# GpSimd makes some of the convolution's products itself, and the first layer norm's sums move between projection units

## The chip, the cores and the metric

One Trainium2 chip, one core. The kernel's time is what the core takes for one launch, in microseconds (us); the numbers shown are the median of several runs. The profile is one execution taken by the hardware profiler, with its own time. TensorE is called PE, VectorE DVE, ScalarE ACT and GpSimd POOL in its rows.

## The reference, cut to what matters

Two transformer blocks over 256 rows of 1024 values, all in float32. The change touches only the token mixer of the first block:

```python
z = rmsnorm(x, mix_norm) @ w_in               # 5376 columns: q, k, v, conv a and b, two gates
q, k = rope(rmsnorm(q, q_norm)), rope(rmsnorm(k, k_norm))
a = sliding_window_attention(q, k, v, sinks) @ attn_proj
u = ca * sigmoid(cb)                          # 1024 channels
u = causal_depthwise_conv(u, dw_w, dw_b)      # 31 taps per channel
c = silu(layernorm(u, g, b)) @ conv_proj
x = x + (sigmoid(ga) * a + sigmoid(gb) * c) @ w_out
```

A layer norm needs the sum over the 1024 channels, then the sum of the squared differences from the mean. The channels lie on the partitions, so both sums are matmuls with a matrix of ones.

## The kernel before, in words

**Weights.** All weights are streamed as units of 128 x 1024 values (512 KB) through a ring of 8 buffers `raw`. A float32 product is made from three fast ones: ScalarE writes a rounded copy `w_hi` (L504), VectorE the rest `w_lo` (L948), and TensorE runs w_hi x a_hi, w_lo x a_hi and w_hi x a_lo for each of two row tiles: 12 matmuls of 512 columns for a unit. SyncE loads unit u once TensorE has done unit u-8. `w.to(n)` in ScalarE's and VectorE's programs writes the parts up to unit n+1, so that these engines write parts some five units ahead of TensorE.

**The mixer's 44 steps.** The columns of w_in are taken in 11 blocks of 4 units: conv 0, conv 1, qkv 0, qkv 1, qkv 2 (half as wide), conv 2, conv 3, gate 0 to 3. TensorE's step s uses unit s; ScalarE's and VectorE's slot s is what their programs do beside it (L716 to L764 and L1356 to L1380). After the last unit of a conv block ScalarE makes its sigmoid (`csg`, L754), VectorE the gated product (`cub`, L1352, function `gated_conv`, in slot 4p+3 of block p), TensorE transposes it two steps on (L1979) and ScalarE copies it to `uT` (L727). `Q1` is slot 20 and `A0` slot 31.

**The heads.** VectorE norms and turns q and k in `shape_heads` in slots 20 to 23: the sums of squares, the inverse root (with a square root on ScalarE, for which two activation tables are loaded), products, the rotation (`rope`, L1334), and last `kdup` (L1340), which TensorE's `k_turn` waits for at step 27. Then `kTz` (L1378) is copied from PSUM in slot 28 (`A0 - 3`), which `q_turn(1)` at step 29 waits for. From step 31 on each step holds a group of attention heads: scores on TensorE, maxima on VectorE (L1226), exponentials on ScalarE, transposes and values on TensorE.

**The 31 taps.** Two of the four pairs of 128-channel chunks (`VECT_CH`) are VectorE's: `conv(n)` adds n taps of one chunk each (L1262, accumulating in PSUM), 124 in all. The others (`POOL_CH`) are made in two steps: ScalarE multiplies (`products(n)`, L673, two instructions for a tap of a pair) into one of two buffers `prod`, and GpSimd adds it to `y` (L485). A product may be written once the add two taps before is done (`pool_step`). `TAPS_IN` and the calls of `products` say how many go into each slot.

**The end.** Eight units of attn_proj (`u_ap`), beside them the last taps; then TensorE sums y (L1993 to L1999), VectorE subtracts the mean, ScalarE squares, TensorE sums the squares (L2005), VectorE and ScalarE make the inverse root and the normed, split input, and TensorE starts conv_proj (`u_cp`); `busy(n, bank)` runs n filler matmuls (L1718) in between. The gates' sigmoids (L774) stand between the last products and the squares. After conv_proj VectorE merges the two branches, and w_out (`u_wo`) follows.

Of the kernel before, what the change touches and what calls it, by code (L numbers as in the profile page):

```python
# [25 lines left out]
P = 128  # L26
S = 256
# [60 lines left out]
def two_blocks(nc, A, consts, out):  # L88
    ctx = ExitStack()
    with ctx:  # L90
# [79 lines left out]
        assert e <= END, (e, END)  # L170
        qT, _, _ = place("qT", [P, KC, S], F32, ARENA)
# [181 lines left out]
        ROOTS = ["heads", "ln", "f2_1", "f2_post0", "mix2_0", "f2_post1", "mix2_1", "gla",  # L353
# [19 lines left out]
        POOL_CH = [0, 4]  # L373
        VECT_CH = [2, 6]
# [10 lines left out]
        A2, OA_AT = 3, 4  # L385
        K_BANK, Q_BANKS = 7, [4, 7, 4, 5]
# [51 lines left out]
        def _(pool):  # L438
# [38 lines left out]

            for g in range(2):
                c = POOL_CH[g]
                for k in range(1, TAPS):  # L480
                    j = (TAPS - 1) * g + k - 1
                    pool.wait_ge(sem("conv_product"), TAP2 * g + 2 * (k + 1))
                    if j >= 1:
                        pool.wait_ge(sem("pool_step"), j)
                    pool.tensor_tensor(y[:, c:c + 2, :], y[:, c:c + 2, :], prod[:, j % 2, :, :], ALU.add).then_inc(sem("pool_step"), 1)  # L485
# [13 lines left out]
        def _(act):  # L499
# [156 lines left out]
            made = [0]  # L656

            def products(n, limit=2 * TAP2):

                for i in range(made[0], min(made[0] + n, limit)):  # L660
                    g, k, half = i // TAP2, i % TAP2 // 2, i % 2
                    c = POOL_CH[g] + half
                    src = uT[:, c, k:k + S]
                    if i % TAP2 == 0:
                        act.wait_ge(sem("uT_ready"), 2 + 2 * g)
                    if k == 0:
                        r = ROW[("dw_b", 0)]
                        ins = act.activation(y[:, c, :], src, ACT.Identity, scale=par[:, c, 0:1], bias=par[:, c, r:r + 1])
                    else:
                        j = (TAPS - 1) * g + k - 1  # L670
                        if j >= 2:
                            act.wait_ge(sem("pool_step"), j - 1)
                        ins = act.activation(prod[:, j % 2, half, :], src, ACT.Copy, scale=par[:, c, k:k + 1])  # L673
                    ins.then_inc(sem("conv_product"), 1)
                made[0] = max(made[0], min(made[0] + n, limit))
# [39 lines left out]

            for slot in range(NMIX):  # L716
# [5 lines left out]
                if slot == Q1:  # L722
                    load_table(ACT.Sqrt)
                if i == 2 and p >= 1 and MIX[p - 1][0] == "conv":
                    j = MIX[p - 1][1]
                    act.wait_ge(sem("conv_turned"), j + 1)
                    act.activation(uT[:, 2 * j:2 * j + 2, TAPS - 1:], ps[:, 4 + j % 2, :].rearrange("p (c n) -> p c n", c=2),  # L727
                                   ACT.Copy).then_inc(sem("uT_ready"), 1)
                if A0 - 3 <= slot <= A0:
                    c = slot - A0 + 3  # L730
                    act.wait_ge(sem("q_turned"), c + 1)
                    act.wait_ge(sem("gqT_ready"), 2)
                    act.activation(qT[:, 2 * c:2 * c + 2, :].rearrange("p c n -> p (c n)"), ps[:, Q_BANKS[c], :], ACT.Copy, scale=gqT)\
# [209 lines left out]
        def _(dve):  # L943
# [412 lines left out]
            for slot in range(NMIX):  # L1356
# [5 lines left out]
                if 1 <= a <= NG:  # L1362
                    take_values(a - 1)
# [843 lines left out]
```

## Time and profile before

| | us |
|---|---|
| median of 3 runs | 1440.61 (1435.54 to 1441.94) |
| the profiled execution's own time | 1436.06 |
| its span in the profile | 1434.3 |
| TensorE busy | 1365.7 (95%) |
| VectorE busy | 961.5 (67%) |
| ScalarE busy | 786.1 (55%) |
| GpSimd busy | 142.2 (10%) |

The mixer of the first block runs from about 212 to 463 us of the span. Busy time of TensorE counts modelled ends of pipelined matmuls, so the gaps between its instructions, and the starts of one and the next, say more than its share. The granted clock is a share of 2.4 GHz, and 0.50 is the level of 1.2 GHz.

### The profile page before, as it was taken

Reading aid. Unit: us, or ns where it says so; the run is one execution under the profiler, and the core shown is the slowest. Engines: PE = TensorE matmul, PEld = TensorE weight load, DVE = VectorE, ACT = ScalarE, POOL = GpSimd, SP = SyncE. Lnnn points to the kernel's source line nnn. Section 1 sums busy time; section 2 is a strip of 40 time slices with the busy share of each in tenths; the row PEclk is TensorE's granted clock in tenths of the full one; section 3 lists DMA queues with packets and bytes.
Section 4 is the critical chain, followed back from the end, with each engine's and each line's share of the span. In section 5 each row is a group of like instructions: output and inputs, shape, how many; then the busy total and the mean of one; then the engine's idle time right before and its main releaser. Section 6 shows DMA issues by size and latency. Waiting matters only on the chain.

```text
span 1434.3 us, 17249 instructions
## 1 busy us (share of the span) xinstructions
PE 1365.7 (95%) x6512; PEld 1124.6 (78%) x6512; DVE 961.5 (67%) x1397; ACT 786.1 (55%) x1249; POOL 142.2 (10%) x166
## 2 busy tenths in 40 slices
PE   7999999849998999999999999999999999999997
PEld 5788788638876888878778878788888888688886
DVE  5767746797867776774768766568776546665543
ACT  5444447858874554444674444676545664754442
POOL 4000102733430000010001000000000000000000
PEclk9999999969999999999999999999999999999999
DMA  9888765613343687875558876555544345556662
GB/s 295 295 265 266 262 187 153 203 44 104 103 133 111 190 273 253 282 264 179 174 186 273 272 261 184 164 170 166 150 146 117 103 146 161 159 179 190 182 188 86
DMA packets 166691, 269.60 MB, mean 188 GB/s; under 512 B 14096, under 2 KB 114616, under 8 KB 166608
## 3 DMA queue, kind: packets, MB, share of 16 engines
q1 hardware_dynamic: 154240, 226.66, 50.8%
q0 software_dynamic: 12064, 41.49, 8.5%
q8 instruction: 52, 0.85, 0.2%
q10 hardware_dynamic: 304, 0.35, 0.1%
q14 instruction: 31, 0.25, 0.1%
HBM read 267.40 MB, written 1.05 MB: 187 GB/s over the span
## 4 chain that ended last, share of the span: by engine, by line
PE 80%; DVE 8%; ACT 6%; DMA 3%; POOL 2%; issue 1%; SPq 0%; DVEq 0%; POOLq 0%; ACTq 0%
PE ps L1645 26%; PE ps L1624 14%; PE ps L1626 14%; PE ps L1625 14%; DVE w_lo L948 3%; DMA raw<-in_ffn_wgu_dram 2%; POOL y L485 2%; ACT w_hi L504 1%; PE ps L1800 1%; PE ps L2059 1%; ACT shift L556 1%; PE ps L1712 1%; DMA raw<-in_ffn_wdown_dram 1%; PE ps L1694 1%; PE ps L1836 1%
## 5 line engine op out<-in xcount | busy, mean ns | idle before, releaser
L948 DVE TENSOR_TENSOR w_lo<-raw,w_hi 128x1024 fp32r<-128x1024 f32 (+2 forms) x431 | 519.9, 1224 | 286.1 <-ACT w_hi L504 284.5
L504 ACT ACTIVATE w_hi<-raw 128x1024 fp32r<-128x1024 f32 (+2 forms) x431 | 447.8, 1053 | 333.5 <-DMA raw<-in_ffn_wgu_dram 94.4
L1624 PE MATMUL ps<-w_hi,a_hi 128*128 128x512 f32 (+1 forms) x1056 | 425.6, 403 | 3.5 <-DVE w_lo L948 1.6
L1626 PE MATMUL ps<-w_hi,a_lo 128*128 128x512 f32 (+1 forms) x1056 | 412.7, 391 | 0.0
L1625 PE MATMUL ps<-w_lo,a_hi 128*128 128x512 f32 (+1 forms) x1056 | 412.2, 390 | 0.0
L1624 PEld LDWEIGHTS ps<-w_hi,a_hi 128*128 128x128 f32 x1056 | 200.1, 190 | 43.5 <-DVE w_lo L948 3.0
L1626 PEld LDWEIGHTS ps<-w_hi,a_lo 128*128 128x128 f32 x1056 | 199.8, 189 | 42.6
L1625 PEld LDWEIGHTS ps<-w_lo,a_hi 128*128 128x128 f32 x1056 | 200.3, 190 | 37.8
L1645 PE MATMUL ps<-w_hi,hid_hi 128*128 128x512 f32 x336 | 104.3, 392 | 0.0
L485 POOL TENSOR_TENSOR y<-y,prod 128x512 f32<-128x512 f32 x60 | 87.7, 1462 | 163.1 <-ACT prod L673 158.6
L1645 PE MATMUL ps<-w_hi,hid_lo 128*128 128x512 f32 x336 | 103.6, 389 | 0.0
L1645 PE MATMUL ps<-w_lo,hid_hi 128*128 128x512 f32 x336 | 103.6, 389 | 0.0
L446 POOL DMA_DIRECT2D ada<-in_w_ada_dram x72 | 38.3, 533 | 485.3 <-DVE acc_m L1164 263.6
L1164 DVE SCALAR_TENSOR_TENSOR acc_m<-ada,csil,acc_m 128x1024 f32<-128x1024 f32 x63 | 80.7, 1280 | 3.8
L1645 PEld LDWEIGHTS ps<-w_hi,hid_lo 128*128 128x128 f32 x336 | 63.1, 188 | 13.3
L1645 PEld LDWEIGHTS ps<-w_lo,hid_hi 128*128 128x128 f32 x336 | 63.1, 188 | 13.2
L1645 PEld LDWEIGHTS ps<-w_hi,hid_hi 128*128 128x128 f32 x336 | 62.4, 188 | 12.5
L673 ACT ACTIVATE prod<-uT,par 128x256 f32<-128x256 f32 x120 | 53.4, 502 | 12.5 <-POOL y L485 12.5
L1645 PE MATMUL ps<-w_hi,a_hi 128*128 128x512 f32 x160 | 50.8, 398 | 0.0
L1645 PE MATMUL ps<-w_lo,a_hi 128*128 128x512 f32 x160 | 49.8, 393 | 0.0
L1645 PE MATMUL ps<-w_hi,a_lo 128*128 128x512 f32 x160 | 49.6, 391 | 0.0
L1262 DVE SCALAR_TENSOR_TENSOR ps<-uT,par,ps 128x256 f32<-128x256 f32 x116 | 48.5, 480 | 0.2
(349 smaller groups left out, 1447.3 us busy)
## 6 DMA issues: line engine op xcount, KB each, us to landing
raw<-in_ffn_wgu_dram SPq DMA_DIRECT2D x176, 256.0 KB, 4.3
raw<-in_w_in_dram SPq DMA_DIRECT2D x88, 512.0 KB, 3.7
raw<-in_w_gu_dram SPq DMA_DIRECT2D x176, 256.0 KB, 3.4
ada<-in_w_ada_dram POOLq DMA_DIRECT2D x72, 512.0 KB, 5.5
raw<-in_ffn_wdown_dram SPq DMA_DIRECT2D x44, 512.0 KB, 4.3
raw<-in_w_dn_dram SPq DMA_DIRECT2D x44, 512.0 KB, 3.6
raw<-in_w_in_dram SPq DMA_DIRECT2D x36, 256.0 KB, 3.1
raw<-in_w_out_dram SPq DMA_DIRECT2D x16, 512.0 KB, 3.7
```

Source lines behind the costliest of these rows:

```text
L446: pool.dma_start(ada[:, i % 3, :], w_ada[k, :, m * D:(m + 1) * D]).then_inc(sem(f"ada_landed{i % 3}"), 16)
L485: pool.tensor_tensor(y[:, c:c + 2, :], y[:, c:c + 2, :], prod[:, j % 2, :, :], ALU.add).then_inc(sem("pool_step"), 1)
L504: act.activation(w_hi[:, u % RING, 0:nk * n], raw[:, u % RING, 0:nk * n], ACT.Copy).then_inc(hi_ready, 1)
L556: act.activation(shift[:, k, :], turn_to(key, t, k), ACT.Identity, scale=modA[:, g, k:k + 1], bias=modB[:, g, k:k + 1]) .then_inc(sem("shi ...
L673: ins = act.activation(prod[:, j % 2, half, :], src, ACT.Copy, scale=par[:, c, k:k + 1])
L948: dve.tensor_tensor(w_lo[:, u % RING, 0:nk * n], raw[:, u % RING, 0:nk * n], w_hi[:, u % RING, 0:nk * n].bitcast(F32), ALU.subtract).then_ ...
L1164: ins = dve.scalar_tensor_tensor(acc_m[:, m % 2, :], ada[:, i % 3, :], csil[:, k:k + 1], acc_m[:, m % 2, :], ALU.mult, ALU.add)
L1262: ins = dve.scalar_tensor_tensor(y[:, c, :] if k == TAPS - 1 else part, src, par[:, c, k:k + 1], part, ALU.mult, ALU.add)
L1624: pe.matmul(dst(t)[:, 0:n], a[0], slot(u, w_hi, kk, n), start=kc == 0, stop=False)
L1625: pe.matmul(dst(t)[:, 0:n], a[0], slot(u, w_lo, kk, n), start=False, stop=False)
L1626: i = pe.matmul(dst(t)[:, 0:n], a[1], slot(u, w_hi, kk, n), start=False, stop=kc == KC - 1)
L1645: i = pe.matmul(ps[:, bank + 2 * t + n, :], a[x_], slot(u, w_, 0, D, 512 * n, 512 * (n + 1)), start=kc == 0 and x_ == 0 and w_ is w_hi, st ...
```

## The change

GpSimd makes the product of some taps itself (`POOL_OWN`), into a buffer of its own, `pown`; ScalarE makes only the others (`FED`). The pairs of chunks are exchanged between VectorE and GpSimd. VectorE begins its taps in slot 7 rather than 11, makes none in slots 16 to 25 and 3 in slots 26 to 30. ScalarE makes 1 product in slots 16 to 25 and 2 in 11 to 15 and 26 to 30, rather than 3 (from slot 7 on). The heads' inverse root is made on VectorE alone, and `shape_heads` is spread over slots 20 to 25; `gated_conv(p)` stands at the head of the next slot, and the transpose of conv 2 at step 27 instead of 25. The sums of y stand behind the fifth unit of attn_proj, those of the squares behind the seventh; the gates' sigmoids stand beside conv_proj.

```diff
+        pown, _, e = place("pown", [P, 2, S], F32, e)
-        POOL_CH = [0, 4]
-        VECT_CH = [2, 6]
+        POOL_CH = [2, 6]
+        VECT_CH = [0, 4]
+        POOL_OWN = {(0, k) for k in [5, 8, 11] + list(range(14, TAPS, 2))} | {(1, k) for k in range(2, TAPS, 4)}
+        FED = [(g, k) for g in range(2) for k in range(TAPS) if k > 0 and (g, k) not in POOL_OWN]
+        UT_BANKS = [4, 5, 5, 5]
+        SUM_AT = 4
...
                     n = (TAPS - 1) * g + k - 1
+                    if (g, k) in POOL_OWN:
+                        own += 1
+                        v = pown
+                        pool.wait_ge(sem("pool_step"), n)
+                        pool.tensor_tensor(pown[:, :, :], uT[:, c:c + 2, k:k + S], par[:, c:c + 2, k:k + 1].to_broadcast([P, 2, S]), ALU.mult)\
+                            .then_inc(sem("pool_product"), 1)
+                        pool.wait_ge(sem("pool_product"), own)
+                    else:
+                        v = prod[:, fed % 2, :, :]
+                        fed += 1
+                        pool.wait_ge(sem("conv_product"), 2 * fed)
+                    if n >= 1 and (g, k) not in POOL_OWN:
+                        pool.wait_ge(sem("pool_step"), n)
+                    pool.tensor_tensor(y[:, c:c + 2, :], y[:, c:c + 2, :], v[:, :, :], ALU.add).then_inc(sem("pool_step"), 1)
...
+            UT_AT = {4 * MIX_AT[("conv", j)] + (8 if j == 2 else 6): j for j in range(4)}
+            PRODUCTS = {slot: 1 if 16 <= slot < 26 else 2 if slot < 31 else 3 for slot in range(11, NMIX)}
...
-                if slot == Q1:
-                    load_table(ACT.Sqrt)
...
-                if slot >= 7:
-                    products(3, TAP2 if slot < 27 else 2 * TAP2)
-                if slot == Q1:
-                    act.wait_ge(sem("heads_summed"), 3)
-                    square_root("heads", rt[:, 1, :], rt[:, 2, :], 1.0 / HD)
-                    load_table(ACT.Sigmoid)
+                if slot in PRODUCTS:
+                    products(PRODUCTS[slot], 0 if slot < 30 else 1)
...
-            for k in range(KC):
+            for k in range(KC - 1):
                 w.to(u_ap + k + 4)
-                products(6)
-            products(2 * TAP2)
-            for half in range(2):
-                for t in range(T):
-                    v = gates[:, t, D * half:D * half + D]
-                    act.activation(v, v, ACT.Sigmoid).then_inc(sem("gates_ready"), 1)
+                products(3 if k < SUM_AT else 2 * len(FED))
             load_table(ACT.Sqrt)
             w.to(u_ap + KC + 3)
...
+            act.activation(st[:, 0, 0, 0:T], rstd[:, :], ACT.Sigmoid)
+            for half in range(2):
+                for t in range(T):
+                    v = gates[:, t, D * half:D * half + D]
+                    act.activation(v, v, ACT.Sigmoid).then_inc(sem("gates_ready"), 1)
+                    w.to(u_cp + 3 + 2 * half + t)
+            load_table(ACT.Silu)
             w.to(u_wo + 2)
...
                 elif part == 1:
-                    inverse_root("heads", rs36[:, :], rt[:, 2, :], 1.0 / HD, small(rt, 36))
+                    rsqrt(rs36[:, :], rt[:, 2, :], 1.0 / HD, small(rt, 36))
+                elif part == 2:
...
-            TAPS_IN = {13: 2, 17: 2, Q1: 2, Q1 + 1: 1, Q1 + 2: 1, Q1 + 3: 1}
+            TAPS_IN = {slot: 0 if slot < 7 or 16 <= slot < 26 else 3 if slot < A0 else 4 for slot in range(NMIX)}
+            TAPS_IN[13] = 2
...
+                if i == 0 and p > 0 and MIX[p - 1][0] == "conv":
+                    gated_conv(p - 1)
+                w.to(M1 + slot + 4)
...
-                if Q1 <= slot < Q1 + 4:
+                if Q1 <= slot < Q1 + 7:
                     shape_heads(slot - Q1)
...
-            for k in range(KC):
+            for k in range(KC - 1):
                 w.to(u_ap + k + 4)
-                conv(6)
+                conv(4)
             conv(2 * TAP2)
...
-            w.to(u_cp + 4)
+            w.to(u_cp + 6)
             dve.wait_ge(used, u_cp)
             dve.wait_ge(sem("gates_ready"), 2 * T)
...
-                if i == 1 and p >= 1 and MIX[p - 1][0] == "conv":
+                if p >= 1 and MIX[p - 1][0] == "conv" and i == (3 if MIX[p - 1][1] == 2 else 1):
...
+                if k == SUM_AT:
+                    pe.wait_ge(sem("conv_step"), 2 * TAP2)
+                    pe.wait_ge(sem("pool_step"), 2 * (TAPS - 1))
+                    for c in range(KC):
+                        i = pe.matmul(ps[:, 6, 0:S], ones, y[:, c, :], start=c == 0, stop=c == KC - 1)
+                    i.then_inc(sem("y_summed"), 1)
+                if k == SUM_AT + 2:
+                    for c in range(KC):
+                        if c % 2 == 0:
+                            pe.wait_ge(sem("ysq_ready"), c // 2 + 1)
+                        i = pe.matmul(ps[:, 7, 0:S], ones, ysq[:, c, :], start=c == 0, stop=c == KC - 1)
+                    i.then_inc(sem("y_summed"), 1)
+            busy(16, 5)
```

## Rows read from the trace of the kernel before

**Rows 1.** The page, part 1: busy us (share of the span) xinstructions.
```profile
PE 1365.7 (95%) x6512; PEld 1124.6 (78%) x6512; DVE 961.5 (67%) x1397; ACT 786.1 (55%) x1249; POOL 142.2 (10%) x166
```

**Rows 2.** Waits from 210 to 480: who waited for whom, us, times, longest.
```profile
PE ps L1979 <- DVE cub L1352: 17.0, 1, 17.0
ACT prod L673 <- POOL y L485: 12.5, 17, 1.4
...
PE ps L1918 <- DVE kTz L1378: 7.1, 1, 7.1
...
PE ps L1624 <- ACT qsq L761: 1.4, 1, 1.4
```

**Rows 3.** Four stretches: us, busy of PE, PEld, DVE, ACT, POOL, clock, DMA.
```profile
327.67:394.40 66.73, 65.68 (x376) 55.99 (x376) 55.68 (x143) 54.99 (x145) 24.71 (x20) 1.00 0.35 103
399.04:438.68 39.64, 35.61 (x155) 27.08 (x153) 24.93 (x40) 27.38 (x43) 11.01 (x7) 0.97 0.35 107
438.68:463.11 24.43, 24.43 (x105) 20.08 (x106) 17.52 (x23) 12.63 (x17) 0.00 (x0) 0.93 0.43 130
275.53:327.67 52.14, 27.65 (x113) 21.92 (x114) 44.31 (x72) 34.72 (x62) 21.97 (x16) 0.74 0.23 70
```

**Rows 4.** TensorE in order of time: start us, us, instruction, [idle before <- releaser].
```profile
280.65 0.39 PE L1625 MATMUL ps<-w_lo,a_hi 128*128 128x512 f32 x1
280.88 0.39 PE L1626 MATMUL ps<-w_hi,a_lo 128*128 128x512 f32 x1
298.28 1.12 PE L1979 MATMUL ps<-const,cub 128*128 128x128 f32 x4 [17.01 <-DVE cub L1352]
...
317.18 1.11 PE L1918 MATMUL ps<-const,qkv 128*128 128x128 f32 x4 [7.14 <-DVE kTz L1378]
```

**Rows 5.** VectorE in order of time, 283 to 317.
```profile
282.99 1.26 DVE L978 TENSOR_SCALAR rt<-rt 128x36 f32<-128x36 f32 x1
...
287.30 1.26 DVE L1325 TENSOR_SCALAR nqs<-rs 128x32 f32<-128x32 f32 x1
...
292.09 3.70 DVE L1334 TENSOR_TENSOR rope<-qkv,const 128x288 f32<-128x288 f32 x4
...
315.35 1.77 DVE L1378 COPY kTz<-ps 64x256 f32<-64x256 f32 x4
```

**Rows 6.** GpSimd in order of time, the same stretch.
```profile
284.44 4.09 POOL L485 TENSOR_TENSOR y<-y,prod 128x512 f32<-128x512 f32 x3 [0.23 <-ACT prod L673]
```

**Rows 7.** Single lines: count, min/median/max ns, first and last start.
```profile
L485 POOL TENSOR_TENSOR y<-y,prod x60: 1263/1296/2163, 237.6 to 412.2; 128x512 f32<-128x512 f32 x60
...
L1334 DVE TENSOR_TENSOR rope<-qkv,const x4: 445/979/1524, 292.1 to 295.3; 128x288 f32<-128x288 f32 x4
```

**Rows 8.** Groups by form, 218 to 440: count, busy us, mean ns, idle before.
```profile
L948 DVE TENSOR_TENSOR w_lo<-raw,w_hi 128x1024 fp32r<-128x1024 f32 x49 | 63.1, 1299 | 19.4 <-ACT w_hi L504 19.3
...
L673 ACT ACTIVATE prod<-uT,par 128x256 f32<-128x256 f32 x120 | 53.4, 502 | 12.5 <-POOL y L485 12.5
L1262 DVE SCALAR_TENSOR_TENSOR ps<-uT,par,ps 128x256 f32<-128x256 f32 x116 | 48.5, 480 | 0.2
...
L515 ACT ACT_TABLE_LOAD x5 | 6.4, 1283 | 0.1
...
L1393 DVE TENSOR_TENSOR y<-y,lnb 128x512 f32<-128x512 f32 x4 | 2.5, 686 | 0.0
```

**Rows 9.** Waits from 327 to 394, the attention steps.
```profile
DVE st L1226 <- PE ps L1873: 10.4, 12, 4.7
```

**Rows 10.** VectorE in order of time, beside attn_proj.
```profile
402.21 2.44 DVE L1262 SCALAR_TENSOR_TENSOR ps<-uT,par,ps 128x256 f32<-128x256 f32 x6
```

**Rows 11.** ScalarE in order of time, beside attn_proj and the layer norm.
```profile
417.75 1.06 ACT L504 ACTIVATE w_hi<-raw 128x1024 fp32r<-128x1024 f32 x1 [1.64 <-DMA raw<-in_conv_proj_dram]
...
420.13 3.90 ACT L774 ACTIVATE gates<-gates 128x1024 f32<-128x1024 f32 x4
```

**Rows 12.** TensorE in order of time, the first matmuls of conv_proj.
```profile
438.68 0.99 PE L1645 MATMUL ps<-w_hi,b_hi 128*128 128x512 f32 x2 [3.78 <-DVE b_lo L1408]
```

More of the change, by code:

```diff
@@ L476, in _ @@
             load_brow(1)
+            pool.wait_ge(sem("par_ready"), 1)
+            fed = own = 0
             for g in range(2):
                 c = POOL_CH[g]
[L480 to L485, printed above, removed]
+                for k in range(TAPS):
+                    if k == 0:
+                        pool.wait_ge(sem("conv_first"), 2 * (g + 1))
+                        continue
+                    n = (TAPS - 1) * g + k - 1
+                    if (g, k) in POOL_OWN:
[12 more added lines that the diff above has]
+                    pool.tensor_tensor(y[:, c:c + 2, :], y[:, c:c + 2, :], v[:, :, :], ALU.add).then_inc(sem("pool_step"), 1)
             pool.wait_ge(used, u_wo)
@@ L654, in take_turned2, with first_tap, products @@
                 act.activation(pt2[:, i % 2, :], ps[:, 5, :], ACT.Copy).then_inc(sem("a2_pt"), 1)
[L656 to L675, printed above, removed]
+            made, begun = [0], [0]
+            def first_tap(g):
+                c, r = POOL_CH[g], ROW[("dw_b", 0)]
+                act.wait_ge(sem("uT_ready"), 3 + 2 * g)
+                for half in range(2):
+                    act.activation(y[:, c + half, :], uT[:, c + half, 0:S], ACT.Identity, scale=par[:, c + half, 0:1],
+                                   bias=par[:, c + half, r:r + 1]).then_inc(sem("conv_first"), 1)
+            def products(n, g_last=1):
+                for _ in range(n):
+                    i = made[0]
+                    if i == 2 * len(FED) or FED[i // 2][0] > g_last:
+                        return
+                    g, k = FED[i // 2]
+                    if begun[0] == g:
+                        first_tap(g)
+                        begun[0] += 1
+                    c, j = POOL_CH[g] + i % 2, i // 2
+                    if i % 2 == 0 and j >= 2:
+                        a, b = FED[j - 2]
+                        act.wait_ge(sem("pool_step"), (TAPS - 1) * a + b)
+                    act.activation(prod[:, j % 2, i % 2, :], uT[:, c, k:k + S], ACT.Copy, scale=par[:, c, k:k + 1]).then_inc(sem("conv_product"), 1)
+                    made[0] += 1
             def weigh(i):
@@ L721, in _ @@
                 w.to(M1 + slot + 4)
-                if slot == Q1:
-                    load_table(ACT.Sqrt)
-                if i == 2 and p >= 1 and MIX[p - 1][0] == "conv":
-                    j = MIX[p - 1][1]
+                if slot in UT_AT:
+                    j = UT_AT[slot]
                     act.wait_ge(sem("conv_turned"), j + 1)
-                    act.activation(uT[:, 2 * j:2 * j + 2, TAPS - 1:], ps[:, 4 + j % 2, :].rearrange("p (c n) -> p c n", c=2),
+                    act.activation(uT[:, 2 * j:2 * j + 2, TAPS - 1:], ps[:, UT_BANKS[j], :].rearrange("p (c n) -> p c n", c=2),
                                    ACT.Copy).then_inc(sem("uT_ready"), 1)
@@ L792, in _ @@
                     act.activation(b_hi[:, c - 1:c + 1, :], cf[:, c - 1:c + 1, :], ACT.Copy).then_inc(sem("b_hi_ready"), 1)
+            act.activation(st[:, 0, 0, 0:T], rstd[:, :], ACT.Sigmoid)
+            for half in range(2):
+                for t in range(T):
[3 more added lines that the diff above has]
+            load_table(ACT.Silu)
             w.to(u_wo + 2)
@@ L1333, in shape_heads @@
                     for n, (half, of) in enumerate([(0, cos), (1, sin), (1, cos), (0, sin)]):
-                        i = dve.tensor_tensor(rope[:, :, n, :, :], z[:, :, :, 8 * half:8 * half + 8], of, ALU.mult)
-                    then(i)
-                else:
+                        dve.tensor_tensor(rope[:, :, n, :, :], z[:, :, :, 8 * half:8 * half + 8], of, ALU.mult).then_inc(sem("rope_made"), 1)
+                elif part == 4:
+                    dve.wait_ge(sem("rope_made"), 4)
                     dve.tensor_tensor(z[:, :, :, 0:8], rope[:, :, 0, :, :], rope[:, :, 1, :, :], ALU.subtract)
@@ L1360, in _ @@
                     heaviest(a)
-                w.to(M1 + slot + 4)
-                if 1 <= a <= NG:
-                    take_values(a - 1)
-                if i == 3 and MIX[p][0] == "conv":
-                    gated_conv(p)
-                if slot in (13, 17):
-                    sum_heads(slot // 4 - 3)
-                if Q1 <= slot < Q1 + 4:
-                    shape_heads(slot - Q1)
-                if i == 1:
-                    take_mods("mix", p)
                 if slot == A0 - 3:
```

57 lines of the change are left out of this document (24 added, 33 removed).

## The prediction

> **What bounds the kernel now.** I read the page's busy shares first: TensorE is busy 95% of the span [rows 1], so only stretches where it stands can give much. The table of waits for the mixer names them: 17.0 us at one transpose (for VectorE's `cub` of conv 2), 7.1 us at `q_turn(1)` (for `kTz`), 1.4 us where qkv 2 is taken from PSUM late [rows 2]. In order of time these are 281.2 to 298.3 and 310.0 to 317.2 [rows 4]. The stretch from step 24 to step 31 lasts 52.14 us at a mean granted clock of 0.74 [rows 3]. The reader should see that TensorE waits there for VectorE, and VectorE for its own queue: every wait named ends at a VectorE instruction. The attention steps are another matter. TensorE is busy 65.7 of 66.7 us at full clock, and VectorE waits for it 10.4 us in 12 times, 5.7 us of it in the 11 waits other than the longest [rows 3, 9]: so much is spare. The stretch from attn_proj to conv_proj's first matmul is 39.64 us [rows 3], of which the 3.78 us before conv_proj are idle [rows 12] and more is filler.
>
> **What a unit costs.** Matmuls of 512 columns start 0.23 us apart at 2.4 GHz [rows 4]; 12 make 2.73 us (0.2275 each). Four transposes I take at 0.36 us.
>
> **Part 1: steps 24 to 31.** TensorE's work there is 7 units (19.1 us) and 7 groups of transposes (2.5), together 21.6; it takes 52.14 [rows 3], and 1.4 more in front of it is the wait for `qsq` [rows 2]. So 31.9 us can be had at most. What changes beside it:
> - VectorE makes no taps in slots 16 to 25. Before it made 11 in slots 16 to 19, 5 in 20 to 23 and 8 in 24 and 25: 24 taps of 0.4 us (six take 2.44 [rows 10]), 9.6 us out of its queue. The 26 put into slots 7 to 15, where it waited for ScalarE, cost nothing: a slot there has a split (1.2), three taps (1.2) and now and then a gated product (0.8), against 2.73.
> - ScalarE drops two table loads of 1.28 us and the square root, makes 40 products fewer at 0.4 us from start to start (0.50 long [rows 8]), and has less of the 12.5 us in which it waited for GpSimd [rows 2]. It then takes qkv 2 from PSUM at about 266, well before step 24 (274.1).
> - VectorE's own chain becomes the bound. From slot 21, which it begins at about 269, to `kdup` it has: split 1.15, inverse root 11 x 0.22 = 2.4, split 1.15, scaling 1.7, split 1.15, rotation 4 x 0.37 = 1.5, gated product 0.8, split 1.15, rest 1.35: 12.4 us, so 281.3. TensorE reaches `k_turn` at 282.2: just hidden.
>
> Not hidden is what GpSimd does to it. Small operations of VectorE with 36 or 32 elements took 1.26 us [rows 5] while GpSimd ran three adds on end [rows 6], and the rotation's four took 445 to 1524 ns [rows 7]; their ends fall on the ends of adds. Taps were not stretched (six in 2.44 us [rows 10], mean 480 ns over the whole mixer [rows 8]). I call it a hold: an add in flight holds a VectorE operation with two inputs from SBUF for between 0 and 1.2 us; I take 0.65, half an add of 1.3 [rows 7]. Six GpSimd operations fall into the chain, 3.9 us: `kdup` at 285.2, TensorE stands 3.0 us. VectorE then needs 8.6 + 0.6 us for two splits more, clearing, 6 taps and the `kTz` copies (1.77 [rows 5]), to 294.4; TensorE reaches `q_turn(1)` at 291.8 and stands 2.6. Step 31 follows at 301.5, and I add 1.5 for the lower clock after the stands (it was 0.74 over this stretch [rows 3]): 303, against 327.67. **Term: -24.7.** Bounds: without any hold 297.5 (-30.2); with 1.2 us each and two stands more 306.5 (-21).
>
> **Part 2: attention, 13 steps.** VectorE and TensorE do the same work as before. GpSimd doesn't: 39 products feed 19.5 adds, and 9 taps of its own bring 18 operations, 37.5 in place of 20 [rows 3]. The new 17.5 at 0.65 hold VectorE 11.4 us; 5.7 of that is spare [rows 9]. **Term: +5.7.** Bounds: 0 (holds fall on taps), +15 (1.2 each: 21 - 5.7).
>
> GpSimd's product is an operation that the trace doesn't show (one operand is one value, repeated). Bounds by the nearest rows: below, ScalarE's 0.50 for half of it, 1.0 together [rows 8]; above, the longest add, 2.16 [rows 7]. I take the add's 1.3, the same shape with two inputs. In the code I count 12 + 8 = 20 such taps, though the change is described with 19. A product of its own also keeps the pace of the sums: from tap 14 of the first pair on, GpSimd has 9 x 2.9 + 8 x 1.46 = 38 us of work from slot 26 to slot 33, where 36.5 are there. ScalarE's products, two ahead, just escape a wait; 0 to 3 us, within the bound above.
>
> **Part 3: attn_proj to conv_proj.** The sums of y wait for all taps and stand after the fifth unit. TensorE ends that unit 14.9 us after it begins attn_proj (5 x 2.73, and 1.2 for a low clock at the start: 0.97 over 39.64 us [rows 3]). VectorE however has taps left: 26 + 15 + 13 x 4 = 93 of 124 are made by slot 43, so 31 are left (14 before). It first splits the activations (2.0 us), then has 7 weight splits at 1.2 and 31 taps at 0.4 [rows 8, 10]: 2.0 + 8.4 + 12.4 = 22.8, with 0.7 for holds of splits 23.5. TensorE stands 8.6 us. (GpSimd, with 5.5 fed and 2 own taps left, 10 operations, ends at about 17.) The sums take 3.5 us at full clock, and about 5.6 after such a stand. Then units 6 and 7 (5.5, the squares ready meanwhile), the squares' sums (3.7) and the same chain as before from there to conv_proj's first matmul (7.2, partly under unit 8 and the filler): 16.4. Start of conv_proj: 23.5 + 5.6 + 16.4 = 45.5, against 39.64 [rows 3]. **Term: +5.9.** Bounds: +4 (no holds, little clock loss), +9.
>
> **Part 4: conv_proj.** The 3.78 us gap in front of it [rows 12] becomes 0.9, so the low clock at its start goes (0.93 over 24.43 us [rows 3]: 3.4 us at 1.2 GHz, which cost 1.7). But the sigmoids (3.90 [rows 11]) now stand behind the last activation, with a table load, and three weight splits between them: `gates_ready` comes 13 us after conv_proj begins (4.3 for the last activations, 1.5, 3.9, three splits of 1.05). VectorE then splits unit 8, makes the gate products and four splits of w_out, and comes to the merge at 21.2; TensorE's second tile wants it at about 20.5, with 1.4 for the first half of the merge: 3.5 us of standing, w_out at 26.1 against 24.43. **Term: +1.7.** Bounds: -1.7, +3.
>
> Nothing after it changes but in time; `pown` lies behind `gates`.
>
> **Sum:** -24.7 + 5.7 + 5.9 + 1.7 = -11.4. From the profiled execution's own 1436.06 (span 1434.3) that is 1424.7; this execution is 4.5 us under the median of the runs, 1440.61. Taken from the median it is 1429; I say 1426, between the two and nearer to the trace. What a measurement can tell from no change is 0.5%, 7.2 us: faster is below 1433.4, slower above 1447.8.
>
> A rule speaks against the choice of GpSimd. The Trainium skill (GPSIMD Engine Reference, section 4.1 Engine selection) gives elementwise products to VectorE, as GpSimd is about twice slower with two inputs; here an add is 1.30 us against 0.69 on VectorE [rows 7, 8], so the rule holds in size, but VectorE is the engine that lacks time. By its remark that one-input work runs near line rate, the product would cost nearer 0.6, as an estimate by that page, and the attention term would fall by some 3 us.
>
> **Rivals.**
> - *No hold.* GpSimd's operations fall beside taps and waits. For it: the mean split was 1.30 us beside GpSimd's 60 adds, where one not held takes about 1.2; against: the stretched rotation. -30.2 + 0 + 5.1 + 1.7 = -23.4: 1412.7 (1415 on the median's side).
> - *All given back.* Each hold is 1.2 us: -21 + 15 + 8 + 1.7 = +3.7: 1440. For it: the rows at 283 to 288, where adds ran on end as they will in slots 26 to 33. The Trainium skill (GPSIMD Engine Reference, section 8 Key points) says that GpSimd shares its SBUF interfaces with VectorE's instructions that have two SBUF inputs; by that rule no split or small operation escapes and this rival would be the likelier; the trace agrees on what is held, and doesn't show how often.
> - *Slower: GpSimd's own product is dear.* Place: slots 26 to 33, where 9 lie in 36.5 us. Each us of a product above 1.46 holds ScalarE 9 us there, and above 1.9 another 8 us in the second pair, since a product waits for the add two before, and TensorE's next transposes wait for ScalarE. It decides from 2.4 us on (9 + 4 us eat the gain). At 3.3: 16.6 + 11.2 - 11.4 = +16, 1452. For it: no row shows the operation. Against: its nearest row is 1.3.
>
> **How the numbers follow.** Forecast 0.52; no hold 0.19; given back 0.19; dear product 0.10. Likeliest alone: 1417 to 1434. The range reaches to the no-hold case and to the given-back case: 1410 to 1440. Faster: 0.49 + 0.19 + 0.04 + 0 = 0.72; same 0.03 + 0.14 + 0.02 = 0.19; slower 0.01 + 0.08 = 0.09.
>
> **What would show it.** Step 31's scores at 299 to 306; no wait for `cub` over 2 us; TensorE standing 6 to 10 us at the first sum of y, released by VectorE's last tap; attention steps of over 5.2 us where GpSimd is busy; GpSimd's products at 1.3 us; conv_proj later after attn_proj than before. Wrong it would be if VectorE's taps end before the fifth unit, or if TensorE still stands long at `cub`.

## The result and the profile after

The changed kernel takes 1445.3 us (median of 14) against 1439.3 for the kernel before: ratio 1.0034, 95% interval 1.0021 to 1.0046, so it is slower by a third of a per cent. I had forecast 1426, with 1440 as the end of the range. One of the 14 executions of the changed kernel took 1969.2 us at a granted clock of 0.65; the ratio and its interval are without it. The profiled execution takes 1446.92 us. The first row below is the page's busy shares, as [rows 1].

```profile
PE 1367.0 (95%) x6504; PEld 1125.0 (78%) x6504; DVE 985.6 (68%) x1403; ACT 767.8 (53%) x1207; POOL 169.6 (12%) x186
```

VectorE is busy 24 us more than before and GpSimd 27 us more, TensorE the same. Next, the windows of four stretches, answering to [rows 3]: step 24 to step 31's scores; the attention steps, from the first scores to attn_proj; attn_proj to conv_proj; conv_proj to w_out. Columns: length, then busy time (and count) of PE, PEld, DVE, ACT, POOL, then clock, DMA share and rate.

```profile
277.72:316.98 39.26, 24.50 (x114) 19.65 (x112) 38.59 (x55) 19.03 (x32) 22.97 (x16) 0.83 0.34 99
316.98:398.20 81.22, 70.71 (x392) 58.68 (x393) 72.00 (x154) 59.26 (x155) 54.46 (x43) 0.98 0.31 91
398.20:447.05 48.85, 35.41 (x147) 27.30 (x145) 35.03 (x57) 21.42 (x37) 16.33 (x10) 0.86 0.27 87
447.05:472.78 25.73, 23.06 (x105) 18.84 (x105) 17.53 (x23) 18.95 (x25) 0.00 (x0) 1.00 0.44 127
```

The stretch that the change aimed at did shrink, from 52.14 us [rows 3] to 39.26, and the two behind it grew by more than as much (the table in the next section has all of them from one starting point). TensorE's long stands in them, from the table of waits:

```profile
PE ps L1935 <- DVE kdup L1370: 13.9, 1, 13.9
...
PE ps L2023 <- DVE y L1290: 12.4, 1, 12.4
...
PE ps L1915 <- DVE qkv L1270: 7.2, 7, 2.6
```

The 17.0 us for `cub` and the 7.1 us for `kTz` [rows 2] are gone, as meant. In their place TensorE stands 13.9 us for `kdup`, 12.4 us for VectorE's last tap, and 7.2 us in seven attention steps. To see why `kdup` is late, read VectorE in order of time (start, length, instruction), here the inverse root and what follows:

```profile
276.00 1.27 DVE L991 TENSOR_SCALAR rt<-rt 128x36 f32<-128x36 f32 x1
277.31 0.18 DVE L992 TENSOR_SCALAR rs<-rt 128x36 int32<-128x36 int32 x1
...
278.48 1.34 DVE L995 SCALAR_TENSOR_TENSOR rt<-rt 128x36 f32<-128x36 f32 x1
279.85 0.20 DVE L996 SCALAR_TENSOR_TENSOR rs<-rt,rs 128x36 f32<-128x36 f32 x1
280.08 1.18 DVE L994 TENSOR_TENSOR rt<-rs 128x36 f32<-128x36 f32 x1
281.30 0.20 DVE L995 SCALAR_TENSOR_TENSOR rt<-rt 128x36 f32<-128x36 f32 x1
281.53 1.33 DVE L996 SCALAR_TENSOR_TENSOR rs<-rt,rs 128x36 f32<-128x36 f32 x1
...
293.24 3.46 DVE L1364 TENSOR_TENSOR rope<-qkv,const 128x288 f32<-128x288 f32 x4
```

and GpSimd beside it:

```profile
277.31 1.08 POOL L497 TENSOR_TENSOR pown<-uT,par 128x512 f32<-128x512 f32 x1
278.47 1.29 POOL L506 TENSOR_TENSOR y<-y,pown 128x512 f32<-128x512 f32 x1
279.90 1.31 POOL L506 TENSOR_TENSOR y<-y,prod 128x512 f32<-128x512 f32 x1
281.52 1.29 POOL L506 TENSOR_TENSOR y<-y,prod 128x512 f32<-128x512 f32 x1 [0.31 <-ACT prod L701]
```

The same operation with 36 elements takes 0.20 or 1.2 us. Each long one ends 0.04 to 0.06 us after a GpSimd operation ends (279.82 after 279.76, 281.26 after 281.21); a short one slips in, GpSimd's next operation begins within 0.31 us of its last one's end, and VectorE's next operation meets it near its start. The root takes 9.4 us where I had 2.4.

### The profile page after: what moved, and what is told of

It is laid out like the page before. It is cut to its first block, busy times and chain, and to the rows that moved or that the text cites. A ratio compares the mean times of both kernels' runs of the same rounds, so it can differ in the third digit from the quotient of the medians.

```text
span 1445.1 us, 17196 instructions
## 1 busy us (share of the span) xinstructions
PE 1367.0 (95%) x6504; PEld 1125.0 (78%) x6504; DVE 985.6 (68%) x1403; ACT 767.8 (53%) x1207; POOL 169.6 (12%) x186
## 3 DMA queue, kind: packets, MB, share of 16 engines
HBM read 267.40 MB, written 1.05 MB: 186 GB/s over the span
## 4 chain that ended last, share of the span: by engine, by line
PE 79%; DVE 11%; ACT 5%; DMA 3%; issue 2%; SPq 0%; DVEq 0%; ACTq 0%
PE ps L1677 24%; PE ps L1656 14%; PE ps L1658 14%; PE ps L1657 14%; DVE w_lo L976 5%; ACT w_hi L525 1%; PE ps L1832 1%; DMA raw<-in_ffn_wgu_dram 1%; PE ps L2083 1%; ACT shift L577 1%; DVE ps L1290 1%; DMA raw<-in_ffn_wdown_dram 1%; PE ps L1744 1%; PE ps L1905 1%; PE ps L1750 1%
## 5 line engine op out<-in xcount | busy, mean ns | idle before, releaser
L976 DVE TENSOR_TENSOR w_lo<-raw,w_hi 128x1024 fp32r<-128x1024 f32 (+2 forms) x431 | 527.0, 1241 | 273.8 <-ACT w_hi L525 271.8
L506 POOL TENSOR_TENSOR y<-y,prod 128x512 f32<-128x512 f32 x40 | 59.4, 1486 | 132.6 <-ACT prod L701 129.4
L653 ACT ACTIVATE hid_hi<-ps 128x512 fp32r<-128x512 f32 x44 | 25.9, 588 | 37.3 <-PE ps L1832 37.3
```

The source lines that it names most:

```text
L506: pool.tensor_tensor(y[:, c:c + 2, :], y[:, c:c + 2, :], v[:, :, :], ALU.add).then_inc(sem("pool_step"), 1)
L653: act.activation(hid_hi[:, 2 * j:2 * j + 2, :].rearrange("p c n -> p (c n)"), ps[:, 4 + j % 2, :], ACT.Copy)\
L976: dve.tensor_tensor(w_lo[:, u % RING, 0:nk * n], raw[:, u % RING, 0:nk * n], w_hi[:, u % RING, 0:nk * n].bitcast(F32), ALU.subtract).then_ ...
```

## The experiments

Two theories at the start. **Hold**: an operation of GpSimd in flight keeps VectorE's operations with two inputs from SBUF waiting until it ends; the prediction's mechanism, but larger than taken. **Chain**: VectorE's own queue is late whatever GpSimd does. Later runs ask how long a hold is, and where GpSimd's work costs least. Ratios are to the kernel before. This table has what the traces show, in us. The first three rows count from the first transpose of conv 0, ahead of all the edits (it starts between 229.2 and 233.7 us in these traces, and that scatter is not the change's).

```
                     before after b_heads b_tiny a_tiny a_half a_quiet a_tail    c1    c2    c3    c4
VectorE's kdup         69.8  66.5    70.7   57.4   51.7   57.2    53.0   66.5  64.2  64.2  59.7  59.7
kTz copied             86.2  73.7    86.7   71.9   58.9   64.8    60.3   73.6  71.4  71.4  67.7  67.7
step 31's scores       98.5  84.1    97.8   83.5   68.2   75.9    70.9   83.8  84.0  83.0  79.4  79.4
scores to attn_proj    71.4  81.2    71.0   70.3   70.8   71.8    83.1   81.4  70.9  71.2  72.6  72.1
attn_proj to conv_proj 39.6  48.9    38.9   38.5   44.3   45.6    57.6   45.8  56.2  53.3  52.4  44.4
conv_proj to w_out     24.4  25.7    24.4   22.8   27.3   25.7    25.8   25.6  24.2  24.4  24.5  24.5
```

**a_tiny: GpSimd's operations made almost nothing** in the changed kernel.
```diff
-pool.tensor_tensor(y[:, c:c+2, :], y[:, c:c+2, :], v[:, :, :], ALU.add)
+pool.tensor_tensor(y[:, c:c+2, 0:2], y[:, c:c+2, 0:2], v[:, :, 0:2], ALU.add)   # its own products likewise
```


> The changed kernel, but every product and add of GpSimd covers 2 of 256 columns: the rest of GpSimd's part of the convolution's sums is left out. Number, order and waits of all operations stay. Theory HOLD (an add or product of GpSimd in flight holds each operation of VectorE with two SBUF inputs until it ends, about 1.1 us and not the 0.65 I took): the operations of 1.1 to 1.3 us among the inverse root's small ones fall to 0.2, the root from 9.4 us to 2.4, kdup from 299.4 to 281-286; TensorE stands under 4 us before k_turn (13.9 now); from conv 2's transposes to step 31's scores 26 to 31 us (now 42.9); attention 66 to 69 us (now 77.1); 1446.9 comes to 1415-1425. Rival CHAIN (VectorE's own queue is late whatever GpSimd does: the root on VectorE, seven slots with a split between the parts): kdup stays at 295 or later, TensorE stands over 9 us before k_turn, the time stays above 1436.

Measured: 1416.1 us, ratio 0.984 (0.982 to 0.987). The same instructions on VectorE:

```profile
272.89 0.18 DVE L991 TENSOR_SCALAR rt<-rt 128x36 f32<-128x36 f32 x1
...
273.79 0.20 DVE L996 SCALAR_TENSOR_TENSOR rs<-rt,rs 128x36 f32<-128x36 f32 x1
274.02 0.20 DVE L994 TENSOR_TENSOR rt<-rs 128x36 f32<-128x36 f32 x1
...
279.25 1.56 DVE L1364 TENSOR_TENSOR rope<-qkv,const 128x288 f32<-128x288 f32 x4
```

The root's eleven are all at 0.18 to 0.20, and the rotation's four take 1.56 together instead of 3.46. TensorE doesn't stand for `kdup` at all, and attention is back at 70.8 us. From the root's first operation to `kdup` it is 10.6 us against 23.4. *Chain* is refuted: VectorE's queue alone would be in time. This run takes away GpSimd's own time too, but little hangs on that: in the changed kernel ScalarE waits for GpSimd 5.2 us in the whole mixer, 1.1 of them ahead of attn_proj, and VectorE isn't idle between the root and `kdup`.

**b_tiny: the same in the kernel before.**
```diff
-pool.tensor_tensor(y[:, c:c+2, :], y[:, c:c+2, :], prod[:, j % 2, :, :], ALU.add)
+pool.tensor_tensor(y[:, c:c+2, 0:2], y[:, c:c+2, 0:2], prod[:, j % 2, :, 0:2], ALU.add)
```


> The kernel before, with GpSimd's adds on 2 of 256 columns (the rest of them is left out). HOLD: VectorE is held there too: the stretch from step 24 to step 31 (52.1 us) loses 6 to 12 us, attention stays at 66 to 67 us as TensorE bounds it, the whole comes to 1424-1430. CHAIN: both stay within 2 us (1434-1437). Together with the changed kernel's run this says how much of the difference between the two kernels comes from holds: by HOLD the changed kernel is at least 5 us faster than the kernel before once both run without them; by CHAIN it is not.

Measured: 1424.6 us, ratio 0.989 (0.987 to 0.992). The kernel before had 15.0 us of holds ahead of step 31 too (98.5 to 83.5), and about 1 in attention. Without any holds the change is worth 8.4 us, the 1424.6 to 1416.1 of the two medians (of four executions each; the two profiled ones are only 4.5 us apart). With them it loses 6.

**a_tail: the tail of the kernel before in the changed one.**
```diff
-                if k == SUM_AT: ...       # sums of y behind the fifth unit
-                if k == SUM_AT + 2: ...   # sums of the squares behind the seventh
+            ...                           # both behind the eighth, filler between
+            sigmoids of the gates ahead of the squares, not behind the last activation
```


> The changed kernel with both sums of the first layer norm behind the eighth projection unit, and the gates' sigmoids ahead of the squares, as in the kernel before. PLACEMENT (the sums stand too early for 31 taps): TensorE works through units 6 to 8 while VectorE makes the taps and stands about 4 us at the first sum (12.4 now); attn_proj to conv_proj 42 to 45 us (now 48.9, before 39.6), conv_proj to w_out 24 to 25; 1446.9 comes to 1439-1442. Rival TAPS (the number of taps left alone sets it, and the place of the sums gives nothing): 48 us, 1445-1447.

Measured: 1441.8 us, ratio to the kernel before 1.0021 (1.0007 to 1.0036). TensorE at the first sum of y:

```profile
421.23 6.15 PE L2020 MATMUL ps<-y,const 128*128 128x256 f32 x16 [4.33 <-DVE y L1287]
```

It stands 4.3 us there instead of 12.4, since units 6 to 8 are done ahead of it; the last tap ends at the same distance (26.3 and 26.2 us after attn_proj's start). The stretch to conv_proj is 3.0 us shorter, of the 9.2 that it had grown by. The sigmoids were moved too, but they lie in a wait there: ScalarE stands 10.0 us for `y` ahead of its first square. So the 3.0 us are the place of the sums. The forecast for the sigmoids was not borne out: conv_proj to w_out is no shorter here.

**b_heads: only the part around q and k, in the kernel before.**
```diff
-inverse_root("heads", ...)    # square root on ScalarE, with two table loads
+rsqrt(rs36[:, :], rt[:, 2, :], 1.0 / HD, small(rt, 36))    # on VectorE; chain over seven slots
```


> The kernel before with only the part around q and k: the inverse root on VectorE in place of ScalarE's square root with its two table loads, and the chain over seven slots. Taps, products and the rest are as before. HOLD: the root's 11 operations are held every other time while GpSimd adds (some 7 us instead of 2.4), so that what ScalarE saves (two table loads, 2.6 us) is eaten: step 24 to 31 at 50 to 58 us (before 52.1), the whole 1434-1442. Rival ROOT GAINS (taking the root off ScalarE is the gain by itself): 45 us or less, 1430 or less.

Measured: 1439.5 us, ratio 1.0004 (0.9989 to 1.0019), no change. The wait for `cub` is 14.9 us against 17.0. The one for `kTz` is 9.7 us against 7.1, so what the first gives the second takes. VectorE's root has five of its eleven operations held and lasts 7.4 us here. Whether the root would have gained anything without the taps that VectorE still makes there, no run shows.

**a_half: GpSimd's operations at half their width** in the changed kernel (diff as in a_tiny, with `0:S // 2`).

> The changed kernel with GpSimd's products and adds on 128 of 256 columns (the other half of its sums is left out), all else kept. In the changed kernel VectorE's chain to kdup had 14 operations held, 13.4 us together, 0.96 each, beside GpSimd operations of 1.05 to 1.4 us that ran on end; with 2 columns none was held. LENGTH (a held operation waits until the GpSimd operation in flight ends, and the two engines then take turns, so a hold is as long as the GpSimd operation): with operations of some 0.6 us the holds are about 0.5 each; kdup comes 57 to 61 us after conv 0's transposes (66.5 at full width, 51.7 at 2 columns), attention 71 to 74.5 us (81.2 and 70.8 from the first score to attn_proj's start), the time 1424-1432. Rival FIXED (a hold costs about 1 us for each GpSimd operation, however short, as long as it isn't trivially short): kdup at 64 or later, attention over 78, time above 1438.

Measured: 1422.9 us, ratio 0.988 (0.986 to 0.990), a little under *length*'s 1424 to 1432; `kdup` at 57.2 and attention at 71.8 us are within it. VectorE, then GpSimd beside it:

```profile
274.57 0.59 DVE L991 TENSOR_SCALAR rt<-rt 128x36 f32<-128x36 f32 x1
275.19 0.18 DVE L992 TENSOR_SCALAR rs<-rt 128x36 int32<-128x36 int32 x1
275.40 0.62 DVE L994 TENSOR_TENSOR rt<-rs 128x36 f32<-128x36 f32 x1
276.06 0.20 DVE L995 SCALAR_TENSOR_TENSOR rt<-rt 128x36 f32<-128x36 f32 x1
276.29 0.62 DVE L996 SCALAR_TENSOR_TENSOR rs<-rt,rs 128x36 f32<-128x36 f32 x1
```
```profile
275.19 0.77 POOL L506 TENSOR_TENSOR y<-y,pown 128x256 f32<-128x256 f32 x1
276.11 0.74 POOL L506 TENSOR_TENSOR y<-y,prod 128x256 f32<-128x256 f32 x1
```

A hold is now 0.42 us (0.62 less 0.20) beside an add of 0.75; it was 0.98 to 1.14 beside 1.3. A hold has the length of the GpSimd operation, less 0.15 to 0.4: *length* holds, *fixed* is refuted. Three held operations in the root are left, not seven, since GpSimd soon had nothing to do. Where it runs on end, nothing is saved: all four operations of the rotation are held here, 0.87 to 1.0 us each instead of 0.45, and take 3.62 us together, no less than the 3.46 at full width, where some escaped.

**a_quiet: no products fed in slots 19 to 26**, so that GpSimd stands still during the chain.
```diff
-PRODUCTS = {slot: 1 if 16 <= slot < 26 else ...}
+PRODUCTS = {slot: 0 if 19 <= slot < 27 else 1 if 16 <= slot < 26 else ...}
```


> The changed kernel with ScalarE feeding no products in slots 19 to 26, so that GpSimd stands still after its backlog while VectorE works through the chain to kdup and kTz; 8 products and the operations behind them come later, at the end of the taps. HOLD: kdup at 52 to 57 us after conv 0's transposes (66.5 now), TensorE's stand before k_turn under 5 us (13.9), first scores at 69 to 75 (84.1 now). Attention stays at 79 to 83 us, attn_proj to conv_proj grows from 48.9 to 50-54 for the work put off, so that the whole comes to 1436-1442. Rival RUSH (what is put off costs as much as it gives): 1444 or more.

Measured: 1444.4 us, ratio to the kernel before 1.0035 (1.0022 to 1.0049). Step 31 comes 13.2 us earlier than in the changed kernel, and `kdup` at 53.0 is 1.3 us from a_tiny's: nearly all the holds that delay it are in the chain, not upstream. But attention takes 1.9 us more, and attn_proj to conv_proj 8.8 us more. There TensorE stands 21.1 us at the sums of y. What was put off came back as a tail; I had allowed for 1 to 5 us of it, and the time is *rush*'s. In attn_proj ScalarE waits 11.6 us for GpSimd, and VectorE 8.0 us for ScalarE's part of the weights, 6.7 of them at once.

**c1: all three findings together**: `POOL_OWN = set()`, the feed silent in slots 21 to 25 and 3 a slot otherwise, 6 a unit in attn_proj, the tail of a_tail.

> A version pointed to by the runs so far: the changed kernel with the tail of the kernel before (both sums behind unit 8, sigmoids ahead of the squares), no products of GpSimd's own (ScalarE feeds all 60 adds), and the feed 3 in each slot but none in slots 21 to 25, six in each unit of attn_proj. HOLD: no GpSimd operation in the chain, kdup at 52 to 58 us after conv 0's transposes, first scores 69 to 76; attention with 20 adds again 71 to 73 us from the first score to attn_proj's start; attn_proj to conv_proj 45 to 50 us (36 products left). Together 1422-1431, faster than both. Rival FEED (ScalarE's 36 products more are late: weight splits or adds are waited for): attention over 75 or attn_proj to conv_proj over 52 us, 1435 or more.

Measured: 1440.0 us, ratio 1.0008 (0.9995 to 1.0021). Attention is at 70.9 us with its 20 adds: the 10 us there were GpSimd's own products and their adds. But *feed* is right about the tail: 56.2 us, with VectorE's splits waiting 12.1 us for ScalarE and ScalarE 8.5 us for GpSimd. And 11.2 us at `kdup` stay. Of the 12.5 us by which it is later than in a_tiny, 4.2 lie behind the split ahead of the root (one operation of the root is held, and a few behind it); 8.3 lie ahead. There slots 16 to 20, fed with 3, left GpSimd a backlog: ScalarE waits for its adds, the weight splits come behind ScalarE's products, and VectorE waits for them; the second split ahead of the root:

```profile
278.65 1.23 DVE L974 TENSOR_TENSOR w_lo<-raw,w_hi 128x1024 fp32r<-128x1024 f32 x1 [3.92 <-ACT w_hi L525]
```

**c2: c1 with 5 taps of VectorE in each attention slot** in place of 4.

> The kernel c1 with five taps of VectorE in each attention slot in place of four: 13 of the 31 taps left for attn_proj are made earlier, where VectorE was busy 55.7 of 66.7 us in the kernel before. SPARE: attention stays within 1 us of c1's, VectorE's last tap comes some 5 us earlier, and attn_proj to conv_proj is 2 to 4 us shorter if VectorE is last there, 0 if GpSimd or ScalarE is: 1419-1429. Rival FULL (VectorE has no room in attention): attention 3 to 6 us longer, the whole no faster than c1.

Measured: 1440.1 us, ratio 0.9992 (0.9978 to 1.0007). *Spare* is right on the place: attention stays at 71.2 us, and VectorE's last tap comes at 24.4 instead of 36.4 us. Now GpSimd is last (TensorE waits 10.6 us for its add), so 3 us are gained there in place of 12. The whole is no faster than c1, as *full* had it, and far from the 1419 to 1429 forecast.

**c3: c2, with GpSimd's work where VectorE isn't bound.**
```diff
-        POOL_CH, VECT_CH = [2, 6], [0, 4]
+        POOL_CH, VECT_CH = [0, 4], [2, 6]
+            PRODUCTS = {slot: 0 if 18 <= slot < 26 else 3 for slot in range(7, NMIX)}
+            # VectorE's taps: 3 in slots 11 to 15, 1 to 20, 0 to 25, 4 to 30, then 5; sums of y in three parts
```


> The kernel c2 rearranged so that GpSimd's 60 adds lie where VectorE is not bound: GpSimd and ScalarE get convs 0 and 2 again, so that the feed starts in slot 7 and not 11 (3 products a slot), stops for slots 18 to 25 (the chain), then 3 a slot; VectorE makes 14 taps in slots 11 to 15, 5 in 16 to 20, none in 21 to 25, 4 a slot to 30, then 5; the sums of y stand in three parts as in the kernel before. HOLD: kdup at 52 to 58 us after conv 0's transposes, first scores at 69 to 75 (84.0 in c1, 98.5 in the kernel before); attention 71 to 72; 36 products are left for attn_proj as in c1, but GpSimd's adds no longer lag, so attn_proj to conv_proj is 41 to 46 us (c1 56.2); the whole 1415-1426. Rival CONSERVED (GpSimd's work always finds something to delay, and what is quiet in one stage comes back in the next): attn_proj to conv_proj 50 or more, 1432 or more.

Measured: 1436.3 us, ratio 0.9979 (0.9966 to 0.9992): the first one faster than both kernels, by little. The root is free of holds, and `kdup` at 59.7; one burst of three adds still falls on the rotation (3.69 us for its four). Attn_proj to conv_proj, 52.4 us, is *conserved*'s number, and the time is too (1432 or more). Its cause is GpSimd itself; first GpSimd, then ScalarE, in one unit of attn_proj:

```profile
391.88 4.80 POOL L506 TENSOR_TENSOR y<-y,prod 128x512 f32<-128x512 f32 x3 [0.53 <-ACT prod L701]
```
```profile
391.31 1.29 ACT L701 ACTIVATE prod<-uT,par 128x256 f32<-128x256 f32 x3
393.84 0.91 ACT L701 ACTIVATE prod<-uT,par 128x256 f32<-128x256 f32 x2 [1.24 <-POOL y L506]
395.27 0.51 ACT L701 ACTIVATE prod<-uT,par 128x256 f32<-128x256 f32 x1 [0.52 <-POOL y L506]
395.69 1.04 ACT L525 ACTIVATE w_hi<-raw 128x1024 fp32r<-128x1024 f32 x1
```

Three adds take 4.80 us, ScalarE waits for them, and the next weight split stands behind its products: a unit takes 5.33 us in place of 2.73.

**c4: c3, with GpSimd's last six adds given to VectorE** as twelve taps in a PSUM bank that is free by then, and two additions to y.
```diff
+        MOVED = 6    # GpSimd's second pair ends at tap 24; VectorE makes 25 to 30 of channels 4, 5
-                products(6)
+                products(4)
```


> The kernel c3 with the last six of GpSimd's 60 adds given up: VectorE makes those taps of channels 4 and 5 in the PSUM bank that its own group has left, and adds them to y at the end (14 operations more on VectorE, 5 to 6 us); ScalarE makes 12 products fewer and 4 a unit in attn_proj in place of 6. GIVE (in c3 attn_proj is bound by GpSimd's 18 adds of 1.6 us, 33 us in all, for which ScalarE and through it the weight splits wait): GpSimd has 12 adds left and ends 20 to 24 us after attn_proj's start, VectorE 23 to 27 us; attn_proj to conv_proj 42 to 46 us (52.4 in c3); before attn_proj nothing moves; the whole 1425-1431. Rival VECTOR (VectorE, held by the adds, is last by as much): 50 us or more, 1434 or more.

Measured: 1426.4 us, ratio 0.9915 (0.9888 to 0.9942), 0.85% faster than the kernel before and 1.3% below the changed one's median. In the windows of c4 the attention steps and attn_proj to conv_proj are:

```profile
309.07:381.13 72.06, 68.22 (x393) 57.54 (x393) 64.37 (x167) 58.71 (x155) 25.61 (x20) 1.00 0.35 102
381.13:425.54 44.41, 36.13 (x156) 26.86 (x153) 32.42 (x60) 30.70 (x51) 18.07 (x11) 0.96 0.31 95
```

What it gains on the kernel before it gains ahead of step 31 (19.1 us), and it gives back 0.7 us in attention and 4.8 us in attn_proj. TensorE still stands 7.1 us for `kdup` in it. Of the 8.0 us by which `kdup` is later than in a_tiny (59.7 against 51.7), 3.1 are holds behind the root: a split of 2.19 us and the rotation's four in 3.69, beside a burst of adds that c3 has too. The other 4.9 lie ahead of the root, which begins 46.0 us after conv 0's transposes (41.1): VectorE has its five taps there, and waits for ScalarE's parts of the weights.

## Why the prediction was wrong

The mechanism was named, its size was not. Each part splits into *free*, the changed kernel without holds (a_tiny) against the kernel before as it is, and *holds*, the changed kernel against a_tiny:

```
                          forecast: free + holds = term      measured: free + holds = term
Part 1, to step 31            -30.2     +5.5      -24.7        -30.3    +15.9     -14.4
Part 2, attention               0       +5.7       +5.7         -0.6    +10.4      +9.8
Part 3, to conv_proj           +5.2     +0.7       +5.9         +4.7     +4.5      +9.2
Part 4, to w_out               +1.7      0         +1.7         +2.9     -1.6      +1.3
Sum                           -23.3    +11.9      -11.4        -23.3    +29.2      +5.9
```

The measured sum, +5.9, is the 6.0 us between the two medians. The two profiled executions are 10.9 us apart; of that 3.7 lie ahead of conv 0's transposes and 1.2 behind the mixer. That the sums of *free* agree to the tenth is luck: its parts miss by 0.1, 0.6, 0.5 and 1.2 us. The column *holds* contains everything that goes with GpSimd's long operations, also what TensorE's stands cost it in clock.

- **The failed step** is in part 1: "an add in flight holds a VectorE operation with two inputs from SBUF for between 0 and 1.2 us; I take 0.65", and "Six GpSimd operations fall into the chain, 3.9 us". Both factors were too small. Half of an add is the mean wait of an operation that comes at any moment. These two engines don't meet at random: GpSimd runs on end, a held operation is released when GpSimd's ends, and VectorE's next or next but one comes just behind the start of the next GpSimd operation. So a hold has nearly the whole length, about 1.0 us in the root's seven. And there were some fourteen in place of six. How the six were found, the prediction doesn't say; an unheld chain of 12.4 us alone has room for nine operations of 1.3. A held chain lasts longer still, and GpSimd, which ran on end with its own products and a backlog, puts more operations into it. From the split ahead of the root to `kdup` the holds make 13.5 us (25.2 us against 11.7 in a_tiny), where I had 3.9; TensorE stood 13.9 us at `k_turn`, not 3.0. The description "with two inputs from SBUF" was too narrow as well: the two operations of 1.26 us in [rows 5] have one.
- **The free chain was right**: forecast 281.3 for `kdup`; a_tiny has it 51.7 us after conv 0's transposes, which is 280.9 in the time of the trace of before (there it begins; it ends at 281.4). Its step 31 comes at 297.4 in that time, forecast 297.5 for no holds.
- **The baseline hid the risk.** The 98.5 us to step 31 in the kernel before had 15.0 us of holds in them. The forecast left 5.5 of them, though the change takes no GpSimd operation out of it: 16 from step 24 on before [rows 3], 16 from step 24 on after, in a shorter stretch.
- **Part 2**: GpSimd ran 43 operations in the 81.2 us, where I had counted 37.5 for 13 steps. VectorE became busy 72.0 of 81.2 us (58.3 of 70.8 with GpSimd tiny), so the spare was soon used up. Here too the 0.65 for a hold was too small: often held is the first small operation of a step behind the scores. Its count and its minimum, median and maximum in ns, before and after, and one of them:

```profile
L1227 DVE TENSOR_TENSOR st<-st,nqs x12: 160/161/424, 329.8 to 387.5; 128x2 f32<-128x2 f32 x8, 128x4 f32<-128x4 f32 x4
L1255 DVE TENSOR_TENSOR st<-st,nqs x12: 160/888/1280, 319.1 to 386.2; 128x2 f32<-128x2 f32 x8, 128x4 f32<-128x4 f32 x4
352.81 1.28 DVE L1255 TENSOR_TENSOR st<-st,nqs 128x2 f32<-128x2 f32 x1
```
In a_tiny none of the twelve is held; one of them:
```profile
328.73 0.16 DVE L1255 TENSOR_TENSOR st<-st,nqs 128x2 f32<-128x2 f32 x1
```
- **Part 3**: the last tap was forecast 22.8 us after attn_proj's start without holds, 22.2 in a_tiny. I added 0.7 for the holds of splits; it was 4.0. A split beside GpSimd took up to 2.19 us, not 1.2. TensorE stood 12.4 us, not "6 to 10".
- **Part 4** came out near its number. How much the sigmoids' place costs stays open: a_tail, with theirs as before, takes 25.6 us and c1, with the same tail, 24.2.
- **The rivals.** "All given back" (1440) had the right mechanism, and should have had most of the chance; even so it was 5 us short, as it left part 1 a gain of 21 us where 14.4 came. "Slower: GpSimd's product dear" is refuted: its own product takes 1.05 us, less than the 1.3 I took (row below, a line's count, then minimum, median, maximum in ns). The products hurt by being there, not by their length. The Trainium skill (SBUF — State Buffer, section "Who interferes with whom") says, of VectorE's two-port modes, that whoever issues first gets the shared ports for the whole instruction and the other blocks fully; of VectorE instructions with two SBUF inputs it says only that they contend with a GpSimd instruction that reads SBUF. The trace shows the full block for a `TENSOR_SCALAR` with one SBUF tensor and for operations with two: each long operation of the root ends within 0.06 us of a GpSimd operation's end. Had I priced part 1 by the full block, each GpSimd operation in its way would have been a whole hold.

```profile
L497 POOL TENSOR_TENSOR pown<-uT,par x20: 1043/1048/2057, 258.7 to 414.7; 128x512 f32<-128x512 f32 x20
```

Right: no wait for `cub`, later attention steps, conv_proj later than before, the release of the sums of y by the last tap. Wrong: step 31 "at 299 to 306" (317.0), the size of TensorE's stand, and the sign.

## What to carry to other kernels

Before work is moved to GpSimd, count its operations in the stretches where VectorE is on the path, and price each at its full length on VectorE's clock; half a length is for engines that meet by chance, and two queues that block each other don't. Put GpSimd's work beside VectorE operations that it can't hold, and see that nothing piles up ahead of the chain that must be short. What is put off comes back at the join, so give the late operations to the engine that has room there: here six adds of 60, given to VectorE, with a feed of 4 a unit in place of 6, made 10 us by the medians (c3 to c4), 8 of them in attn_proj to conv_proj. The two were changed together, so what each is worth isn't shown.

## What the runs showed of the hardware

- In the root a hold lasts as long as the GpSimd operation, less 0.15 to 0.4 us: 0.98 to 1.14 us beside adds of 1.3, 0.72 and 0.89 beside products of 1.05 to 1.08, 0.42 beside 0.75, none beside operations on 128x4 elements.
- It is not only for operations with two tensors from SBUF: a `TENSOR_SCALAR` of 36 floats from SBUF to SBUF took 1.27 us against 0.18. Taps, which read one tensor from SBUF and one from PSUM, were not held: four in 1.66 us beside GpSimd's adds in the changed kernel (below), 1.66 in a_tiny, while the split behind them took 2.19 us.

```profile
401.27 1.66 DVE L1290 SCALAR_TENSOR_TENSOR ps<-uT,par,ps 128x256 f32<-128x256 f32 x4
402.84 2.19 DVE L976 TENSOR_TENSOR w_lo<-raw,w_hi 128x1024 fp32r<-128x1024 f32 x1
```
```profile
400.56 5.62 POOL L506 TENSOR_TENSOR y<-y,prod 128x512 f32<-128x512 f32 x3 [3.81 <-ACT prod L701]
```

- GpSimd is held as well. In a_tiny an add on 128x4 elements took 1.26 us beside VectorE's split (1.21 us, from 283.92), where others took 0.20:

```profile
283.65 0.20 POOL L497 TENSOR_TENSOR pown<-uT,par 128x4 f32<-128x4 f32 x1
283.93 1.26 POOL L506 TENSOR_TENSOR y<-y,pown 128x4 f32<-128x4 f32 x1
```
